# Two attention layers of a 1-core block: jobs in pairs, a bias by matmuls, products between the runs

## The chip, the core and the metric

One NeuronCore of a Trainium2 chip runs the whole program. Its engines work side by side and meet through semaphores: PE (TensorE, matmuls and transposes into PSUM), DVE (VectorE), ACT (ScalarE), POOL (GpSimd) and SP (SyncE, which here issues the loads). The metric is the time of one execution in microseconds of the device, as the median of several runs. Lower is better.

## What is computed

Two blocks follow each other on 512 tokens of width 1024: a first block (a gated mixer, a recurrent mixer, and a mixture of experts behind each), then a second block of two layers. The change touches the attention of the second block's two layers. Shortened to it:

```python
h = rmsnorm(x, ln1_g[i]) @ w_in[i]
(fq, fk, fv, ff, dq, dk, dv, c_q, c_kv, k_r) = jnp.split(h, split_points, axis=-1)
# third kind of jobs below: 4 heads of 64, causal, decay bias cum[q] - cum[k]
logf = log_sigmoid(ff + f_bias);  cum = jnp.cumsum(logf, axis=1)
o_fox  = softmax(fq @ fk.T / 8 + where(k <= q, cum[q] - cum[k], NEG)) @ fv
# second kind: 4 heads, two score maps each (widths 64 and 64), values of 128
o1, o2 = softmax(q1 @ k1.T / 8 + alibi_and_chunk_mask) @ v, softmax(q2 @ k2.T / 8 + ...) @ v
o_diff = rmsnorm(o1 - lam * o2, norm_g) * (1 - lam_init)
# first kind: 4 heads of 64 + 32 rotated, chunk mask
o_mla  = softmax(q @ k.T * 96 ** -0.5 + chunk_mask) @ v
x = x + concatenate([o_fox, o_diff, o_mla]) @ w_o[i]
```

Everything is fp32. A feed-forward part follows each attention.

## The kernel before

The program is written out engine by engine. For each stage there is one function per engine (`tensor()`, `scalar()`, `vector()`, `gpsimd()` inside `attention`, L1792), and the order of the lines in it is the order of the engine's queue. Nothing is reordered by a scheduler. Results go from PE to the others through eight PSUM banks taken in turn (`Banks.take`, L131): PE waits there until the bank's last reader has released it.

**Dense products.** Weights arrive as raw fp32 units, and each half of a unit is split into a high part (ACT, L263) and a low part (DVE or POOL, L271), six halves ahead. A product (L593 with features as output rows, L595 with tokens as output rows) is then three matmuls for each piece. In the attention they are, by the names of their keys: `mla` (L528), `dq`, `dk`, `dv`, `fv`, `fqk`, and `atto`, the product with `w_o` in two column halves (`(atto, 0)` at L595, `(atto, 1)` at L615).

**Jobs.** A job is one head, one query block of 128 and, in the second kind, one of the two maps. The blocks come in the order `BLOCKS = (3, 1, 2, 0)`, and block `qc` sees keys in `128 * (qc + 1)` columns. There are 16 jobs of the first kind (`mla`), 32 of the second (`diff`), 16 of the third (`fox`). A job is
- scores: one fp32 matmul of 96 rows (first kind) or 64 rows (the others), L1870;
- DVE adds the bias and scales while it copies the scores out of PSUM (L2063), then takes the maximum (L2064);
- ACT takes the exponential and its sum (L1964);
- PE transposes the result (L1876), ACT copies it to SBUF (L1972), PE multiplies with the values (L1884);
- DVE scales by the reciprocal sum (L2069, and L2077, L2081 and L2083, or L2086).

`pipeline` (L1847) runs the jobs of one kind with a lag of three: on PE the transposes of job m-3, the scores of job m, the values of job m-4. Each kind has its own run, which fills and drains. `dv` stands inside the second kind's run. `fv` and `fqk` stand between the second and the third run.

**The third kind's bias.** The forget logits come as four extra columns of `fv`. After that product DVE takes their log-sigmoid (L743) and PE sums it up over tokens (L1927, 20 short matmuls). The sums are turned to a row (L1935), and for each head a matmul with 4 rows spreads them over the partitions (L1867). ACT copies that, adds the query's own sum (L1961), POOL masks the diagonal block (L2173), and only then DVE adds it to the scores. L501 turns finished output columns to features for the last product; ACT and DVE split them (L506, L513).

**The second kind's norm** is on ACT 16 squares (L2023) and a root (L406), and on DVE 16 scalings (L2136) and 4 more (L2143), placed between the second and third run, in DVE's queue ahead of the log-sigmoid.

## Time and profile before

| | us |
|---|---|
| median of 3 runs | 2784.52 (2782.84 to 2785.44) |
| the profiled execution, its own time | 2782.48 |
| its span | 2781.3 |

| engine | busy us | share of the span |
|---|---|---|
| PE, matmuls | 2669.2 | 96% |
| PE, weight loads | 1851.0 | 67% |
| DVE | 1220.8 | 44% |
| ACT | 928.7 | 33% |
| POOL | 368.2 | 13% |

### The profile page before, as it was taken

What the parts mean: (1) busy time and instruction counts of PE and PEld (TensorE: products, weight loads), DVE (VectorE), ACT (ScalarE), POOL (GpSimd) and SP (SyncE); (2) the same over time, 40 slices, a digit from 0 to 9 for tenths busy, and PEclk for the clock granted to TensorE, in tenths of its full rate; (3) what the DMA queues carried; (4) which work ended last, traced back from release to release, by engine and by line L of the source; (5) the groups of instructions that cost most, each with busy time, mean ns of one, the idle gap of its engine ahead of it and who ended that gap; (6) DMA issues with size and microseconds to landing.
All of it is one profiled execution on the core that took longest, in us unless ns stands there. A gap on an engine that the chain in (4) does not pass through costs nothing. (4 is left out here: it accounts for less than half of the span.)

```text
span 2781.3 us, 33208 instructions
## 1 busy us (share of the span) xinstructions
PE 2669.2 (96%) x13232; PEld 1851.0 (67%) x13232; DVE 1220.8 (44%) x2353; ACT 928.7 (33%) x1770; POOL 368.2 (13%) x197
## 2 busy tenths in 40 slices
PE   7989999999978999999799999999999999999999
PEld 6865444454856444544487768888888776888887
DVE  2542232333655232322445733562554573356254
ACT  4431111112373111111345543442344554344233
POOL 3200000001230000000120111221222011122122
PEclk9999999999989999999999969999999995999999
DMA  5139999998215999999621001322132100132212
GB/s 210 64 125 411 421 421 421 421 421 346 76 46 218 420 421 421 421 421 421 249 88 61 32 30 61 107 95 87 61 110 94 61 33 30 61 106 94 89 61 83
DMA packets 136893, 543.62 MB, mean 195 GB/s; under 512 B 16672, under 2 KB 28192, under 8 KB 87456
## 3 DMA queue, kind: packets, MB, share of 16 engines
q1 hardware_dynamic: 127120, 536.94, 49.2%
q10 hardware_dynamic: 9616, 4.51, 0.6%
q8 instruction: 108, 1.77, 0.3%
q14 instruction: 49, 0.40, 0.0%
HBM read 539.32 MB, written 2.10 MB: 195 GB/s over the span
## 5 line engine op out<-in xcount | busy, mean ns | idle before, releaser
L593 PE MATMUL ps<-w,w 128*128 128x512 f32 x2976 | 678.8, 390 | 2.6 <-POOL w L271 2.6
L593 PEld LDWEIGHTS ps<-w,w 128*128 128x128 f32 x2976 | 558.2, 188 | 120.0 <-POOL w L271 3.4
L271 POOL TENSOR_TENSOR w<-w,w 128x1024 fp32r<-128x1024 f32 (+3 forms) x139 | 335.7, 2425 | 2152.8 <-ACT w L263 2152.8
L1345 PE MATMUL ps<-w,w 128*64 128x512 f32 x2048 | 451.6, 594 | 1.8 <-issue 1.8
L595 PE MATMUL ps<-w,w 128*128 128x512 f32 (+1 forms) x1872 | 413.5, 383 | 17.4 <-issue 15.2
L595 PEld LDWEIGHTS ps<-w,w 128*128 128x128 f32 x1872 | 342.3, 190 | 86.6 <-issue 19.9
L263 ACT ACTIVATE w<-w 128x1024 fp32r<-128x1024 f32 (+3 forms) x260 | 252.4, 999 | 414.3 <-PE ps L595 182.0
L271 DVE TENSOR_TENSOR w<-w,w 128x1024 fp32r<-128x1024 f32 (+3 forms) x121 | 192.5, 1597 | 371.1 <-ACT w L263 368.7
L1345 PEld LDWEIGHTS ps<-w,w 128*64 128x64 f32 x2048 | 146.0, 137 | 285.6 <-issue 285.6
L1597 DVE TENSOR_TENSOR X<-ps,X 128x512 f32<-128x512 f32 x256 | 163.0, 682 | 163.3 <-PE ps L1381 162.3
L1367 PE MATMUL ps<-w,w 128*64 128x512 f32 x1024 | 226.8, 595 | 0.8 <-ACT w L1431 0.8
L2281 DVE SCALAR_TENSOR_TENSOR w<-ps,PK,w 128x511 f32<-128x511 f32 (+1 forms) x176 | 131.9, 749 | 75.5 <-ACT w L2237 72.4
L1367 PEld LDWEIGHTS ps<-w,w 128*64 128x64 f32 x1024 | 70.6, 137 | 139.8 <-issue 138.9
L1884 PEld LDWEIGHTS ps<-w,w 128*128 128x128 f32 x640 | 97.8, 224 | 56.9 <-ACT w L1972 28.0
L1320 PE MATMUL ps<-w,w 128*128 128x256 f32 x1024 | 130.8, 287 | 4.9 <-DVE w L1568 4.9
L1320 PEld LDWEIGHTS ps<-w,w 128*128 128x128 f32 x1024 | 129.7, 195 | 7.6 <-DVE w L1568 5.1
L1585 DVE TENSOR_TENSOR w<-ps,w 128x512 f32<-128x512 f32 x32 | 34.8, 1086 | 212.0 <-PE ps L1345 212.0
L615 PE MATMUL ps<-w,w 128*128 128x512 f32 x528 | 122.0, 390 | 0.0
L1884 PE MATMUL ps<-w,w 128*128 128x64 f32 (+1 forms) x640 | 115.5, 321 | 4.6 <-ACT w L1972 4.1
L1380 PE MATMUL ps<-w,w 128*128 128x512 f32 x256 | 111.9, 437 | 4.6 <-DVE w L1604 4.6
L1604 DVE SCALAR_TENSOR_TENSOR w<-ps,w,w 128x512 fp32r<-128x512 f32 x64 | 45.1, 747 | 159.0 <-ACT w L1476 159.0
L615 PEld LDWEIGHTS ps<-w,w 128*128 128x128 f32 x528 | 98.8, 188 | 20.3
(247 smaller groups left out, 2505.5 us busy)
## 6 DMA issues: line engine op xcount, KB each, us to landing
w<-in_moe_w_gate SPq DMA_DIRECT2D x128, 1024.0 KB, 13.9
w<-in_moe_w_up SPq DMA_DIRECT2D x128, 1024.0 KB, 16.6
w<-in_moe_w_down SPq DMA_DIRECT2D x128, 1024.0 KB, 13.1
w<-in_w_up SPq DMA_DIRECT2D x40, 1024.0 KB, 5.1
w<-in_w_down SPq DMA_DIRECT2D x20, 1024.0 KB, 5.0
w<-in_w_in SPq DMA_DIRECT2D x16, 1024.0 KB, 5.0
w<-in_ab_w_in SPq DMA_DIRECT2D x10, 1024.0 KB, 5.2
w<-in_c_w_in SPq DMA_DIRECT2D x8, 1024.0 KB, 5.0
```

What stands on the lines that cost most here:

```text
L263: up(self.whi, self.S.e.activation(hi, raw, ACT.Copy))
L271: up(self.wlo[self.low[s][0]], lane.e.tensor_tensor(lo, raw, hi.bitcast(F32), ALU.subtract))
L593: ins = pe.matmul(bank[:, :], wp[:, k, P * o:P * o + P], ap(k0 + k), start=first, stop=stop)
L595: ins = pe.matmul(bank[:, 0:width], ap(k0 + k)[:, P * o:P * o + P], wp[:, k, :], start=first, stop=stop)
L615: ins = pe.matmul(bank_of(o)[:, 0:width], ap(k)[:, P * o:P * o + P], wp, start=(k == 0 and pi == 0), stop=(hi is rows[-1][0] and pi == 2))
L1320: i = pe.matmul(bank[:, 256 * k:256 * k + 256], HB[part][:, c, t:t + P], SELR[:, c, :], start=(part == 0 and c == 0), stop=(part == 1 and ...
L1345: ins = pe.matmul(bank[64 * e:64 * e + 64, :], XG[p % 3][:, 4 * u + k, 64 * e:64 * e + 64], w[e][:, k, :], start=(u == 0 and k == 0), stop ...
L1367: ins = pe.matmul(two[n][64 * e:64 * e + 64, :], HDT[:, 2 * u + k, 64 * e:64 * e + 64], w[e][:, k, 512 * n:512 * n + 512], start=(u == 0 a ...
L1380: pe.matmul(bank[:, :], s_, YH[:, 512 * n:512 * n + 512], start=True, stop=False)
L1597: up(bx.free, dve.tensor_tensor(x, bank[:, :], x, ALU.add))
L1884: ins = pe.matmul(bank[:, 0:dv], PTB[m % 2][:, P * j:P * j + P], vals(j), start=(j == 0), stop=(j == qc))
L2281: ins = dve.scalar_tensor_tensor(y[:, d:T], bank[:, 0:T - d], col("conv_w_2", 132 * i + 44 * tap + f), y[:, d:T], ALU.mult, ALU.add)
```

## The change

1. **Two jobs at a time.** `pipeline` goes in steps of two jobs: the values of job 2p-5, the transposes of 2p-4 and 2p-3, the scores of 2p and 2p+1, the values of 2p-4. The two score matmuls follow each other. In the second kind the two are the two maps, in rows 0 to 63 and 64 to 127. The third kind's jobs are reordered so that a pair is two heads, in the same two row halves. The first kind's pairs use 96 rows each.
2. **One run for the first two kinds**, with `dv` at step 10 and `fqk` at step 24, after the last scores of the second kind and before its last transposes and values.
3. **The third kind's bias by matmuls.** The sums are written as three bf16 parts each, with ones beside them, turned to rows once for all heads, and a bf16 matmul of 6 rows adds `cum[q] - cum[k]` into the same PSUM bank as the scores. A bf16 matmul of the identity with a causal block of 0 and -1e30 adds the mask. ACT scales the queries by 1/8 as it copies them. DVE takes the maximum straight from PSUM and ACT the exponential straight from PSUM. L1867, L1935, L1961, L2173 and the third kind's part of L2063 are gone.
4. **The forget logits ride with `mla`** (420 columns, a second small load of 16 KB for each unit). Log-sigmoid and sums come before `dk`; the parts are made by DVE before it splits `dk`'s next weights; 8 bf16 transposes and one ACT copy follow the transposes of the first kind.
5. **Products between.** `fv` (256 columns) stands at step 2 of the third kind. The norm of the second kind is in DVE's queue ahead of that step. Six output features are turned in steps 3 to 5. The last three steps of the third kind stand in the middle of `(atto, 0)`, whose row halves are taken in the order (1, 0), while four PSUM banks are held.

```diff
+            for p in steps:
+                if p in at_step:
+                    at_step[p]()
+                if first_values:
+                    values_of(2 * p - 5)
+                for m in (2 * p - 4, 2 * p - 3):
+                    if 0 <= m < len(jobs):
+                        turn(m0 + m, jobs[m])
+                if 2 * p < len(jobs):
+                    scores(m0 + 2 * p, jobs[2 * p:2 * p + 2])
+                if not first_values:
+                    values_of(2 * p - 5)
+                values_of(2 * p - 4)
...
+        def two_kinds(engine, dv, fqk):
+            n = M_FOX // 2
+            pipeline(mla_jobs + diff_jobs, 0, engine, {M_DIFF // 2 + 2: dv, n: fqk}, range(n + 3))
+
+        def third_kind(engine, fv, o_feature):
+            at_step = {2: fv}
+            for n in range(3):
+                at_step[3 + n] = lambda n=n: o_feature(FEATURES_OUT[2 * n:2 * n + 2])
+            pipeline(fox_jobs, M_FOX, engine, at_step, range(len(fox_jobs) // 2))
...
-            bank = banks.take(bsc)
-            n = P * (qc + 1)
-            up(bsc.full, pe.matmul(bank[:, 0:n], q, k[:, 0:n], start=True, stop=True))
+            taken = [banks.take(kind) for _ in two]
+            for bank, (qc, _, _, q, k, _, _) in zip(taken, two):
+                n = P * (qc + 1)
+                ins = pe.matmul(bank[:, 0:n], q, k[:, 0:n], start=True, stop=not fox)
+                if not fox:
+                    up(bsc.full, ins)
+            if fox:
+                for bank, (qc, _, h, _, _, _, _) in zip(taken, two):
+                    n, of_head = P * (qc + 1), slice(32 * h, 32 * h + 6)
+                    pe.matmul(bank[:, 0:n], turned_q[of_head, P * qc:P * qc + P], turned_k[of_head, 0:n],
+                              start=False, stop=False)
+                for bank, (qc, _, _, _, _, _, _) in zip(taken, two):
+                    n = P * (qc + 1)
+                    up(bfs.full, pe.matmul(bank[:, n - P:n], CTB[:, 0, :], CTB[:, 1, :], start=False, stop=True))
...
+            def rest(unit):
+                if unit == 1:
+                    banks.held = bx.banks[-NT:]
+                    rest_of_third(engine)
+                    PE.wait_ge(bo.free, M_FOX + len(fox_jobs))
+                    tensor_o_features(FEATURES_OUT[6:])
+                    banks.held = ()
...
+            if kind == "fox":
+                bank = bfs.next(V)
+                up(mx, dve.tensor_reduce(AT[:, m % 8:m % 8 + 1], bank[:, 0:n], AX, ALU.max, negate=True))
+                return
```

On PE, in the second kind, before (L1870 scores, L1884 values, L1876 transposes; an `x2` is two matmuls in one row):

```order
L1870 MATMUL ps<-w_22528_11034,w_20480_11032 128x512
L1884 MATMUL ps<-w_16384_11035,w_14336_11026 128x128 x3
L1876 MATMUL ps<-CT,w_12288_11025 128x128
L1870 MATMUL ps<-w_22528_11034,w_20480_11032 128x512
L1884 MATMUL ps<-w_16384_11035,w_14336_11026 128x128 x3
L1876 MATMUL ps<-CT,w_12288_11025 128x128
```

And now (L1924 scores, L1954 values, L1946 transposes):

```order
L1924 MATMUL ps<-w_22528_11038,w_20480_11036 128x512 x2
L1954 MATMUL ps<-w_16384_11039,w_14336_11030 128x128 x6
L1946 MATMUL ps<-CT,w_12288_11029 128x128 x2
L1924 MATMUL ps<-w_22528_11038,w_20480_11036 128x256 x2
L1954 MATMUL ps<-w_16384_11039,w_14336_11030 128x128 x2
```

The two maps' scores now stand next to each other, and so do their values and transposes.

On PE, around the last scores of the third kind and the middle of `(atto, 0)`, now (L1930 the bias of 6 rows, L1934 the mask, L602 a dense product, w_20480 queries and keys, w_22528 the third kind's values):

```order
L1924 MATMUL ps<-w_20480_11042 128x128 x2
L1930 MATMUL ps<-junk 128x128 x2
L1934 MATMUL ps<-CTB 128x128 x2
L1954 MATMUL ps<-w_22528_11043,w_14336_11030 128x64 x2
L602 MATMUL ps<-w_32768_62,w_0_74 128x512
...
L1954 MATMUL ps<-w_22528_11043,w_14336_11030 128x64 x2
L1946 MATMUL ps<-CT,w_12288_11029 128x128 x6
L1954 MATMUL ps<-w_22528_11043,w_14336_11030 128x64 x6
L1946 MATMUL ps<-CT,w_12288_11029 128x128 x2
L1954 MATMUL ps<-w_22528_11043,w_14336_11030 128x64 x2
L508 MATMUL ps<-CT,w_8192_11028 128x128 x8
```

48 of `(atto, 0)`'s 96 matmuls stand between the third kind's last scores and its drain; before, all 96 followed the drain.

On DVE, from the last jobs of the second kind to the first of the third, before (L412 to L2143 the norm, L271 weight splits, L2146 on the log-sigmoid):

```order
L2081 TENSOR_TENSOR AT<-AT,LS 128x1
L2083 SCALAR_TENSOR_TENSOR w_8192_11024<-ps,AT,w_18432_11036 128x128
L412 RECIPROCAL SM<-SM 128x16
L2136 SCALAR_TENSOR_TENSOR w_8192_11024<-w_8192_11024,SM,dnB 128x128 x16
L2143 TENSOR_SCALAR w_8192_11024<-w_8192_11024 128x512 x4
L271 TENSOR_TENSOR w_37888_70<-w_28672_51,w_36864_64 128x1024
L271 TENSOR_TENSOR w_41984_72<-w_30720_52,w_40960_66 128x1024
L2146 TENSOR_TENSOR sb_cum<-w_22528_11039,fgB 128x16
```

And now (L2145 maxima of the third kind, L419 to L2261 the norm, L277 weight splits, L2166 reciprocals):

```order
L2178 TENSOR_TENSOR AT<-AT,LS 128x1
L2180 SCALAR_TENSOR_TENSOR w_8192_11028<-ps,AT,w_18432_11040 128x128
L2145 TENSOR_REDUCE AT<-ps 128x1 x4
L419 RECIPROCAL SM<-SM 128x16
L2254 SCALAR_TENSOR_TENSOR w_8192_11028<-w_8192_11028,SM,dnB 128x128 x16
L2261 TENSOR_SCALAR w_8192_11028<-w_8192_11028 128x512 x4
L277 TENSOR_TENSOR w_33792_68<-w_24576_49,w_32768_62 128x1024
L277 TENSOR_TENSOR w_37888_70<-w_26624_50,w_36864_64 128x1024
L2166 RECIPROCAL AT<-AT 128x1 x2
L2145 TENSOR_REDUCE AT<-ps 128x1 x2
```

The log-sigmoid has left this place; four maxima of the third kind stand before the norm, and the maxima of its third pair behind it and behind two weight splits.

## Rows read from the trace of the kernel before

**Rows 1.** The page: span, PE, and the slices' granted clock in tenths.

```profile
span 2781.3 us, 33208 instructions
PE 2669.2 (96%) x13232; PEld 1851.0 (67%) x13232; DVE 1220.8 (44%) x2353; ACT 928.7 (33%) x1770; POOL 368.2 (13%) x197
PEclk9999999999989999999999969999999995999999
```

**Rows 2.** Busy time by stretch: stretch, length, engines, granted clock, DMA share, GB/s.

```profile
1466.02:1491.29 25.27, 22.90 (x153) 17.72 (x153) 19.29 (x63) 16.00 (x49) 0.00 (x0) 1.00 0.14 51
1491.29:1514.83 23.54, 23.54 (x103) 18.61 (x102) 6.40 (x12) 6.33 (x12) 1.30 (x1) 1.00 0.12 45
1514.83:1568.96 54.13, 53.30 (x298) 35.95 (x299) 42.75 (x138) 30.78 (x92) 2.36 (x1) 1.00 0.07 20
1568.96:1602.22 33.26, 33.26 (x194) 29.51 (x194) 22.33 (x54) 17.89 (x50) 7.38 (x3) 1.00 0.27 94
1602.22:1609.09 6.87, 4.54 (x42) 4.20 (x40) 3.36 (x8) 3.72 (x7) 2.37 (x1) 1.00 0.24 56
1609.09:1668.83 59.74, 57.50 (x177) 36.54 (x177) 22.43 (x67) 28.05 (x72) 4.67 (x16) 0.54 0.03 13
1668.83:1692.15 23.32, 23.32 (x97) 19.16 (x97) 4.99 (x6) 3.18 (x3) 2.39 (x1) 0.93 0.14 46
```

**Rows 3.** The second layer's last two stretches; ten microseconds of the first's third kind.

```profile
2304.27:2364.01 59.74, 56.60 (x176) 35.68 (x177) 22.42 (x67) 28.05 (x72) 4.67 (x16) 0.55 0.03 10
2364.01:2387.89 23.88, 23.88 (x96) 19.58 (x97) 4.98 (x6) 3.18 (x3) 2.39 (x1) 0.91 0.14 45
...
1640.00:1650.00 10.00, 10.00 (x26) 5.08 (x25) 3.32 (x12) 5.12 (x14) 1.00 (x4) 0.50 0.00 1
```

**Rows 4.** Who waited for whom on PE, 1461 to 1670 us.

```profile
PE ps L1867 <- DVE tr L2158: 2.3, 1, 2.3
...
PE ps L1876 <- ACT w L1964: 1.4, 1, 1.4
...
PE ps L595 <- DVE w L513: 0.7, 1, 0.7
```

**Rows 5.** PE's timeline where the first kind's run begins.

```profile
1461.49 3.65 PE L501 MATMUL ps<-CT,w 128*96 128x128 f32 x32
1466.02 2.17 PE L1870 MATMUL ps<-w,w 96*128 96x512 f32 x6 [0.87 <-DVE w L2128]
```

**Rows 6.** One head of each kind: first kind, then second, by stretch.

```profile
1476.30:1481.83 5.53, 5.53 (x40) 4.34 (x39) 4.89 (x17) 3.83 (x13) 0.00 (x0) 1.00 0.01 3
...
1524.38:1538.45 14.07, 14.07 (x77) 9.22 (x77) 11.83 (x38) 7.81 (x25) 0.00 (x0) 1.00 0.01 2
```

**Rows 7.** PE's timeline: a lone score matmul, and three at the run's start.

```profile
1524.38 1.12 PE L1870 MATMUL ps<-w,w 64*128 64x512 f32 x2
1525.43 0.82 PE L1884 MATMUL ps<-w,w 128*128 128x128 f32 x5
...
1491.29 1.55 PE L1870 MATMUL ps<-w,w 64*128 64x512 f32 x6
1492.77 22.06 PE L595 MATMUL ps<-w,w 128*128 128x512 f32 x96
```

**Rows 8.** DVE's groups in the second kind's head: busy, mean, idle before, releasers.

```profile
L2063 DVE SCALAR_TENSOR_TENSOR w<-ps,w 128x512 f32<-128x512 f32 (+3 forms) x8 | 3.9, 489 | 1.8 <-PE ps L1870 1.5 <-DVE w L2051 0.2
```

**Rows 9.** PE's timeline: the sums ahead of the third kind.

```profile
1602.22 2.29 PE L1927 MATMUL ps<-sb_cum,CT 128*128 128x4 f32 x20
```

**Rows 10.** The page's kind of group, whole trace, shapes apart: a small bf16 matmul.

```profile
L1331 PE MATMUL ps<-w,w 128*128 128x128 bf16 x128 | 12.4, 219 | 0.0
```

**Rows 11.** DVE's timeline: end of the rotation, and the norm.

```profile
1460.41 0.64 DVE L2122 COPY w<-w 128x128 f32<-128x128 f32 x4
...
1576.31 0.25 DVE L412 RECIPROCAL SM<-SM 128x16 f32<-128x16 f32 x1 [6.49 <-ACT SM L406]
1576.60 8.58 DVE L2136 SCALAR_TENSOR_TENSOR w<-w,SM,dnB 128x128 f32<-128x128 f32 x16
```

More of the change, by code:

```diff
@@ L193, in add @@
             self.n_dense += 1
-        self.count[slot] += 16 * len(parts)
+        self.count[slot] += 16 * sum(len(pieces) for _, _, pieces in parts)
         u = Unit(len(self.units), parts, split, len(self.halves), slot, self.count[slot], self.holder[slot])
@@ L1862, in tensor_scores, with pipeline, values_of @@
-        def tensor_scores(m, job):
-            qc, kind, h, q, k, _, _ = job
-            if kind == "fox" and qc == BLOCKS[0]:
-                PE.wait_ge(crow, 1)
-                bank = banks.take(ba)
-                up(ba.full, pe.matmul(bank[:, :], cst("sel")[0:4, P * h:P * h + P], CROW[0:4, :], start=True, stop=True))
-            bank = banks.take(bsc)
-            n = P * (qc + 1)
-            up(bsc.full, pe.matmul(bank[:, 0:n], q, k[:, 0:n], start=True, stop=True))
+        def pipeline(jobs, m0, engine, at_step, steps):
+            scores, turn, values = engine
+            first_values = turn is tensor_turn
+            def values_of(m):
+                if 0 <= m < len(jobs):
+                    values(m0 + m, jobs[m])
+            for p in steps:
[4 more added lines that the diff above has]
+                for m in (2 * p - 4, 2 * p - 3):
+                    if 0 <= m < len(jobs):
+                        turn(m0 + m, jobs[m])
[4 more added lines that the diff above has]
+                values_of(2 * p - 4)
@@ L1929, in tensor @@
             up(bv.full, ins)
-            PE.wait_ge(o_done, 4)
-            tensor_o_features((6, 7, 2, 3))
-            PE.wait_ge(cum, 2)
-            bank = banks.take(bv)
-            for c in range(NT):
-                ins = pe.transpose(bank[0:4, P * c:P * c + P], CU[:, c, :], ident)
-            up(bv.full, ins)
-            PE.wait_ge(ba.free, 30 + 8)
-            pipeline(fox_jobs, M_FOX, tensor_scores, tensor_turn, tensor_values, lambda: tensor_o_features((4, 5)))
-            PE.wait_ge(bo.free, M_FOX + len(fox_jobs))
@@ L1940, in tensor @@
-            tensor_o_features((0, 1))
-            place = {k: n for n, k in enumerate((6, 7, 2, 3, 4, 5, 0, 1))}
-            def ready(k):
-                PE.wait_total(bf.free, mark["o"] + 1 + max(place[x] for x in range(k)))
-            tensor_out(("atto", i), H, ready, ahead=lambda: tensor_half(next_rows, 0))
-        def scalar_scores(m, job):
+            tensor_product(("dk", i), ALL4, 512, H, ba, feature=True)
+            PE.wait_ge(q1k1, 1)
+            tensor_features(lambda c, h: Q1[:, c, 96 * h:96 * h + 96], 4, lambda k: bv if k % 2 else ba, rows=96)
@@ new lines, in tensor @@
+            tensor_features(lambda c, h: K1[:, c, h, :], 4, lambda k: bv if k % 2 else ba, rows=96)
+            PE.wait_ge(cum_parts, 1)
+            PE.wait_total(ctb, 2)
+            bank = banks.take(ba)
+            for j in range(2):
+                for c in range(NT):
+                    ins = pe.transpose(bank[:, :].bitcast(BF16)[:, T * j + P * c:T * j + P * c + P], CM6[:, j, c, :], CTB[:, 0, :])
+            up(ba.full, ins)
+            PE.wait_ge(ba.free, 10 + 8 + 4 + 4)
+            PE.wait_ge(bv.free, 2 + 4)
@@ L1950, in scalar_scores, with scalar_exp @@
+            tensor_out(("atto", i), [lambda k, f=f: f(ROWS_OUT[k]) for f in H], ready, rest,
+                       ahead=lambda: tensor_half(next_rows, 0))
+        def scalar_scores(m, two):
+            scalar_exp(m, two[0])
+            scalar_exp(m + 1, two[1])
+        def scalar_exp(m, job):
             qc, kind, h = job[0], job[1], job[2]
             n = P * (qc + 1)
+            p = PB[m % (LAG + 1)]
+            scores = p
             if kind == "fox":
-                if qc == BLOCKS[0]:
-                    bank = ba.next(S)
-                    S.wait_ge(fox_m, 4 * h)
-                    bank_to(NB, bank[:, :])
-                    S.wait_total(ba.free, ba.free.n)
@@ L1958, in scalar_scores @@
[L1958 to L1962 removed]
+                scores = bfs.next(S)
+                S.wait_ge(bpt.full, m - LAG)
             S.wait_ge(mx, m + 1)
[L1964 to L1965 removed]
+            up(bfs.free if kind == "fox" else ex,
+               act.activation(p[:, 0:n], scores[:, 0:n], ACT.Exp, bias=AT[:, m % 8:m % 8 + 1],
+                              accum_out=AT[:, 8 + m % 8:9 + m % 8]))
@@ L2450, in constants @@
     put("pri8", np.tile(8 - np.arange(8, dtype=np.float32), (P, 1)))
-    sel = np.zeros((4, 4, P), np.float32)
-    for h in range(4):
-        sel[h, h, :] = -1.0
-    put("sel", sel.reshape(4, 512))
+    put("causal", np.where(j <= p, 0.0, NEG).astype(np.float32))
     return c
```

246 lines of the change are left out of this document (137 added, 109 removed).

## The prediction, made before the run

> **What bounds the kernel now.** I read the page first: PE is busy 96% of 2781.3 us, and its clock row shows two dips in the second half [rows 1]. Everything the change moves lies in two stretches, one for each layer, so the next view is the busy time by stretch, from the first kind's first scores to the end of `(atto, 0)` and the first part of `(atto, 1)` [rows 2]. The seven stretches sum to 226.1 us. The reader is to see that PE is busy for nearly all of each, and that one stands out: 59.74 us for the third kind at a granted clock of 0.54, in the second layer 59.74 us at 0.55 [rows 3]. Within it, 10.00 of 10.00 us are busy at 0.50: PE is the bound there, at half speed. DVE and ACT are busy 22.43 and 28.05 us of it. In the other kinds PE is the bound at full clock: a head of the second kind takes 14.07 us with PE busy throughout and DVE 11.83 us, a head of the first 5.53 us with DVE 4.89 us [rows 6]. PE's waits are short [rows 4].
>
> **Start of the runs: +3.2 us a layer.** The 20 sum matmuls (2.29 us [rows 9]) now stand ahead of `dk`; they are taken out again below, so only the place changes. What is new is on DVE. Its rotation ends at 1461.05 [rows 11], just before PE's turns at 1461.49 [rows 5], and behind it now come a copy, three memsets and nine small steps, by DVE's small steps of about 0.2 us some 3 us, and only then two weight splits and the four copies for which PE waits 0.87 us [rows 5]. PE comes there 2.2 us later than before, so about 1 us more is seen, and with it 8 bf16 transposes (0.1 us each by 12.4/128 [rows 10]). Bounds: +0.5 to +3 beside the 2.2. I take 1.0. The log-sigmoid goes into a time in which DVE waits for PE: nothing. Queued behind it are DVE's splits for `dk`, needed 20 us later. The extra 16 KB loads go through SP's queue well ahead: nothing. POOL loses 16 masks, and two casts at the start hide in its wait for weights.
>
> **First and second kind: -10.3 us a layer.** Do two fp32 matmuls of 64 rows in different halves really run together? The old order has this once: three score matmuls (512, 512 and 256 columns) take from 1491.29 to 1492.77, 1.48 us, where a lone 512 takes 1.05 us [rows 7]. In sequence they would take 1.05 + 1.05 + 0.5 = 2.6. So the second one costs almost nothing. A head has 2 x 1280 columns, by 1.05 us for 512 some 5.3 us; half, 2.6, goes, and some 0.1 us of change-over for each job: 2.9. PE would need 11.2 us. But DVE has its own work: of the 14.07 us it waits 1.5 for scores [rows 8], so it needs 12.6. DVE becomes the bound, and the gain is 1.5 a head, 6.0 a layer (bounds: 0 if the longer loop of two jobs makes PE and DVE wait for each other, 11.6 if PE stayed the bound). The first kind's pairs have 96 rows and can't run together; its 5.53 stays. Its drain goes: the stretch has 25.27 - 22.90 = 2.4 us of idle time [rows 2], 1.4 of it at the start, which stays; 1.0 goes. The second kind's drain (last 3.3 us of its 54.13, behind the last scores) moves behind `fqk` and is counted there. Together 6.0 + 1.0 + 3.3.
>
> **From `fv` to the end of the 96th `atto` matmul: -30.1 us a layer.** Before: 33.26 + 6.87 + 59.74 + 23.32 = 123.2 us [rows 2]. After, on PE, all at full clock:
> Dense work: 33.26 + 22.4 = 55.7 (the 23.32 had some 0.9 us of half clock).
> The second kind's drain: 3.3, and about 1.9 more since ACT first empties `fqk`'s banks and splits a weight half: 5.2.
> The third kind's scores: four heads of 1280 columns in pairs, 2 x 2.6, and change-overs: 5.9. Transposes and values are those of the first kind: 5.53 less its scores (1280 columns at 1.05 for 512, less 0.1 each: 2.3) is 3.2 for a head, four times 13.0.
> The added bias and mask. A dense product streams 512 columns in 22.06/96 = 0.23 us [rows 7]; 5120 bias columns are then 2.3 us if each runs alone. 16 mask matmuls of 128 columns are 1.6 us by 0.10 each [rows 10]. Bounds 2.7 (pairs of bias matmuls together) to 6 (each at the fp32 rate). I take 3.9, as these are bf16.
> Eight turned features, by 3.65/8 = 0.46 us each for 4 transposes [rows 5]: 3.7.
> Changing between 128, 64 and 32 rows: a lone 64-row score costs 0.1 us more than a 96-row one would; two or three changes for each of 8 steps: 2.0.
> Waits: PE behind ACT's copies of `fv` 1.1; scores of step 3 behind step 2's exponentials, whose maxima wait on DVE behind the norm, 0.5; in the middle of `(atto, 0)` for copies 1.0; for the last values and features 1.1 as before (0.7 of it in [rows 4]): 3.7.
> Sum: 55.7 + 5.2 + 5.9 + 13.0 + 3.9 + 3.7 + 2.0 + 3.7 = 93.1.
> Gone from the path are the sums (2.3), the row and the spreading matmuls, the wait of 2.3 us behind them [rows 4], and above all the half clock.
> The norm is the place to watch. Before, `fqk` hid it. Now squares and root on ACT (DVE waited 6.49 us for them), then 8.58 us and four smaller scalings on DVE [rows 11] and two splits stand ahead of the maxima of step 2: about 19 us after the drain. PE has 3.1 us of scores, 11.5 of `fv`, 1.1 of waiting and 3.5 of step 2: the cover is just long enough. If `fv` were not there, 10 us would show.
>
> **The sum.** 3.2 - 10.3 - 30.1 = -37.2 for the first layer. In the second the last stretch is 0.6 us longer, at half clock for longer [rows 3]: -37.8. Together -75.0, from the profiled execution's own 2782.5: 2707.5. The median of the runs is 2 us above that execution, so I forecast **2710 us**.
>
> **A rule of the skill against the rows.** The third kind stays at 0.50 for 10 us in which PE is never idle [rows 3]. Behind that stands what the Trainium skill says (TensorE: Matmul & The Clock Gate, "What's actually happening"): the throttled state is the default and activity releases it. By that rule the full clock would be sure after the change, as PE stays busy; the trace does not agree that being busy is enough. The first kind, with much the same matmuls, keeps 1.00 [rows 2].
>
> **Rivals.**
> A. *The third kind falls to the half clock again.* For: before, it is entered at 1.00 and loses it after short matmuls of 4 columns or 4 rows and a wait of 2.3 us; in the second layer with less waiting too. Against: it now comes out of 22 us of `fqk`, is cut by `fv` and `(atto, 0)`, has no 4-row matmuls, and is like the first kind. From step 2 to 7 PE has about 19 us of work; doubled, less 2 us of waits that vanish: +17 a layer, 2743 us. In one layer only: 2726. 20%.
> B. *No gain from pairs.* The loop is longer (maximum of both, exponential of both, then transposes), or the matmuls don't run together in this stream, which is also how the change could fail to do what it says. Then 6.0 of the jobs and 2.6 of the third kind's scores don't come, and waits of 2 us do: 10.6 a layer, 2730. Speaks against: [rows 7]. 12%.
> C. *More than forecast:* DVE's 12.6 has slack in it (it is busy 11.83), bias pairs run together, fewer change-overs: 0.8 x 4 + 1.2 + 1 + 1 = 6 a layer, 2697. 9%.
> D. *Slower.* The clock is lost at the start of the first kind's run, behind 40 transposes and a longer wait for DVE, and PE then goes on at 0.50. First kind 22 more, the second kind from `dv` on 22.2 us a head against 12.6, in some 3.5 heads 34 more, third 17: 73 against 38 gained, 35 a layer, 2853 us. It decides as soon as more than 38 us of PE's full-clock work a layer run at half. The rows speak against: from 1461.49 on PE turns 32 blocks and waits 0.87 and 1.4 us, and the clock stays 1.00 [rows 2, 4, 5]. The Trainium skill (same page, "Part 4: PE-mode transpose") says that full clock does not engage in transpose mode; by that rule the added transposes would count for D, and the trace so far does not bear it out there. 4%.
>
> **How the numbers follow.** Forecast 55%, A 20%, B 12%, C 9%, D 4%. The forecast's own bounds (start +2, jobs 3 either way, bias -1.2 to +2 a layer) reach from 2699 to 2725. With A, B and C the range is 2695 to 2745; D is out, and the far ends of A and B with it. All but D are faster by far more than 0.2% (5.6 us, about what a measurement of this kernel can tell from no change): faster 95%, within 0.2% 1%, slower 4%.
>
> **What the profile of the changed kernel will show.** A head of the second kind near 12.6 us with DVE idle for less than 0.5 and PE idle now and then, each pair of 512 columns in about 1.1 us; the first scores about 3 us later after `dk`; the third kind at 1.00, some 22 us of PE between `fv` and `(atto, 0)`; no wait above 2 us at step 2 or 3. I am wrong if PEclk still dips there (A), if the head stays near 14 us (B), or if PE waits long for DVE's maxima behind the norm.

## The result, and the profile after

| | us |
|---|---|
| before, median of 4 runs | 2784.57 (2782.84 to 2785.44) |
| after, median of 4 runs | 2748.92 (2748.84 to 2750.51) |
| ratio | 0.9874, 95% interval 0.9857 to 0.9891 |
| forecast | 2710, range 2695 to 2745 |

The change made the kernel 35.6 us faster, where 75 were forecast; the time lies 4 us outside the range. In what follows, *before* and *after* are the two kernels and the traces of their profiled executions. That of after has a span of 2749.0 us against 2781.3 [rows 1].

These lines of after's page answer to [rows 1]. Both dips of PEclk in the second half are gone:

```profile
span 2749.0 us, 33272 instructions
PE 2610.8 (95%) x13288; PEld 1825.9 (66%) x13288; DVE 1201.3 (44%) x2337; ACT 910.1 (33%) x1740; POOL 361.4 (13%) x167
PEclk9999999999989999999999999999999999999999
```

The first layer's stretches in after answer to [rows 2]: first kind up to `dv`, `dv`, second kind up to `fqk`, `fqk`, drain and first third-kind scores, `fv` to the last scores, `(atto, 0)` with the third kind's rest. Columns as there (length; PE, PEld, DVE, ACT, POOL busy; granted clock; DMA):

```profile
1472.09:1502.81 30.72, 25.30 (x158) 18.72 (x159) 22.22 (x68) 18.65 (x54) 0.00 (x0) 1.00 0.10 36
1502.81:1526.44 23.63, 23.63 (x98) 19.07 (x97) 3.41 (x9) 5.75 (x10) 2.40 (x1) 0.93 0.13 44
1526.44:1580.42 53.98, 43.06 (x272) 31.09 (x271) 36.94 (x121) 28.77 (x82) 1.27 (x1) 0.91 0.07 21
1580.42:1602.32 21.90, 21.90 (x100) 18.11 (x99) 3.45 (x10) 5.00 (x10) 1.29 (x1) 1.00 0.15 49
1602.32:1609.75 7.43, 6.26 (x45) 4.12 (x44) 3.46 (x12) 4.45 (x18) 2.35 (x1) 1.00 0.24 73
1609.75:1647.88 38.13, 35.38 (x263) 29.44 (x262) 24.67 (x65) 26.73 (x79) 5.63 (x2) 0.91 0.20 70
1647.88:1679.07 31.19, 29.58 (x134) 24.20 (x134) 7.89 (x20) 6.39 (x13) 2.37 (x1) 0.89 0.11 34
```

The third kind has left the half clock: 0.91 where [rows 2, 3] have 0.54 and 0.55. But in the second kind PE was busy for 53.30 of 54.13 us before; now it is idle for 11 of 53.98 us. The prediction's three terms, by the starts of the same operations in both traces:

| term | forecast | layer 1 | layer 2 |
|---|---|---|---|
| `mla` to the first scores | +3.2 | +4.2 | +4.1 |
| first and second kind, with `dv` | -10.3 | +5.4 | +4.4 |
| `fqk` or `fv` to the 96th `atto` | -30.1 | -24.5 | -27.7 |

With 1.9 us lost before the first layer's attention this makes -32.2; the spans differ by -32.3. (The other 3.3 of the 35.6 are how each profiled execution lies to its median.) The middle row is the failed step.

Who waited for whom on PE in after's first layer, 1472 to 1681 us (columns: us in total, times, longest). Before, the only waits above a microsecond were 2.3 and 1.4 [rows 4]:

```profile
PE ps L1946 <- DVE w L2180: 8.8, 8, 1.8
PE ps L1946 <- ACT w L2048: 3.8, 7, 1.1
PE ps L1946 <- DVE w L2183: 3.1, 5, 1.3
```

L1946 is the transpose of a job's exponentials, and L2180 and L2183 are DVE scaling *values*. A transpose needs no values. What it needs is a PSUM bank. PE's timeline where a head of the second kind begins, layer 2 of after:

```profile
2230.23 1.13 PE L1924 MATMUL ps<-w,w 64*128 64x512 f32 x4
2231.29 1.60 PE L1954 MATMUL ps<-w,w 128*128 128x128 f32 x12
2232.73 0.27 PE L1946 MATMUL ps<-CT,w 128*128 128x128 f32 x1
2234.77 0.30 PE L1946 MATMUL ps<-CT,w 128*128 128x128 f32 x1 [1.77 <-DVE w L2180]
2235.00 0.70 PE L1924 MATMUL ps<-w,w 64*128 64x256 f32 x4
```

and DVE's in the same time (L2160 bias, L2161 maximum):

```profile
2233.49 0.69 DVE L2161 TENSOR_REDUCE AT<-w 128x1 f32<-128x512 f32 x1
2234.09 0.15 DVE L2178 TENSOR_TENSOR AT<-AT,LS 128x1 f32<-128x1 f32 x1
2234.28 0.35 DVE L2180 SCALAR_TENSOR_TENSOR w<-ps,AT,w 128x128 f32<-128x128 f32 x1
...
2235.74 0.43 DVE L2160 SCALAR_TENSOR_TENSOR w<-ps,w 128x256 f32<-128x256 f32 x1 [0.72 <-PE ps L1924]
```

A step takes six banks of the eight in turn: values 2p-5, transposes 2p-4 and 2p-3, scores 2p and 2p+1, values 2p-4. Eight takes before the second transposes lie the values of job 2p-7. PE takes the values of 2p-5 at the *start* of a step; the code has DVE scale them at the *end* of its step, behind both score tiles. So PE's transpose at 2234.77 waits for DVE's end at 2234.63, and DVE then waits 0.72 us for PE's next scores: they go in turns. In the next two steps of this head PE waits for DVE again at the same place, 1.22 and 0.63 us; in the fourth its wait is one of 0.34 us for ACT. The theory BANK of the runs below is this loop.

### The profile page after: what moved, and what is told of

Read it like the earlier page. It is cut to its first block, busy times and chain, and to the rows that moved or that the text cites. A ratio compares the mean times of both kernels' runs of the same rounds, so it can differ in the third digit from the quotient of the medians.

```text
span 2749.0 us, 33272 instructions
## 1 busy us (share of the span) xinstructions
PE 2610.8 (95%) x13288; PEld 1825.9 (66%) x13288; DVE 1201.3 (44%) x2337; ACT 910.1 (33%) x1740; POOL 361.4 (13%) x167
## 4 chain that ended last, share of the span: by engine, by line
PE 88%; DVE 6%; issue 3%; ACT 2%; DMA 0%; POOL 0%; SPq 0%; DVEq 0%; ACTq 0%
PE ps L600 24%; PE ps L1362 16%; PE ps L602 14%; PE ps L1384 8%; PE ps L1337 5%; PE ps L622 4%; PE ps L534 3%; PE ps L1397 3%; PE ps L1398 2%; PE ps L1924 1%; PE ps L1954 1%; DVE w L2160 1%; PE ps L535 1%; PE ps L1946 1%; PE ps L452 1%
## 5 line engine op out<-in xcount | busy, mean ns | idle before, releaser
L600 PEld LDWEIGHTS ps<-w,w 128*128 128x128 f32 x2976 | 560.2, 188 | 120.2 <-POOL w L277 3.4
L277 POOL TENSOR_TENSOR w<-w,w 128x1024 fp32r<-128x1024 f32 (+2 forms) x139 | 337.7, 2439 | 2228.7 <-ACT w L269 2228.7
L602 PE MATMUL ps<-w,w 128*128 128x512 f32 (+1 forms) x1872 | 416.3, 384 | 17.8 <-issue 15.2
L602 PEld LDWEIGHTS ps<-w,w 128*128 128x128 f32 x1872 | 343.8, 191 | 86.8 <-issue 19.5
L269 ACT ACTIVATE w<-w 128x1024 fp32r<-128x1024 f32 (+2 forms) x260 | 252.7, 1001 | 436.1 <-PE ps L600 196.4
L277 DVE TENSOR_TENSOR w<-w,w 128x1024 fp32r<-128x1024 f32 (+2 forms) x121 | 201.6, 1674 | 387.7 <-ACT w L269 385.1
L1337 PE MATMUL ps<-w,w 128*128 128x256 f32 x1024 | 131.3, 288 | 4.9 <-DVE w L1585 4.9
L1337 PEld LDWEIGHTS ps<-w,w 128*128 128x128 f32 x1024 | 130.2, 196 | 7.6 <-DVE w L1585 5.1
L622 PEld LDWEIGHTS ps<-w,w 128*128 128x128 f32 x528 | 98.7, 188 | 20.3
L1493 ACT ACTIVATE w<-ps,w 128x512 fp32r<-128x512 f32 x64 | 40.6, 684 | 204.0 <-PE ps L1384 204.0
L534 PE MATMUL ps<-w,w 128*128 128x256 f32 x768 | 99.9, 294 | 8.3 <-POOL w L277 6.7
```

The costliest lines, as they stand in the source:

```text
L269: up(self.whi, self.S.e.activation(hi, raw, ACT.Copy))
L277: up(self.wlo[self.low[s][0]], lane.e.tensor_tensor(lo, raw, hi.bitcast(F32), ALU.subtract))
L534: return pe.matmul(bs[o][:, t], w[:, P * o:P * o + P], a(k)[:, t], start=first, stop=stop)
L600: ins = pe.matmul(bank[:, :], wp[:, k, P * o:P * o + P], ap(k0 + k), start=first, stop=stop)
L602: ins = pe.matmul(bank[:, 0:width], ap(k0 + k)[:, P * o:P * o + P], wp[:, k, :], start=first, stop=stop)
L622: ins = pe.matmul(bank_of(o)[:, 0:width], ap(k)[:, P * o:P * o + P], wp, start=(k == 0 and pi == 0), stop=(hi is rows[-1][0] and pi == 2))
```

## The experiments

Each kernel is the changed one with the edit shown, unless said otherwise; `...` stands for lines left out. Each quoted passage is what was expected before the run. Every median is that of the kernel's own runs; before stood at 2784.1 to 2785.0 beside them.

### Values first on DVE

```diff
-                if first_values:
-                    values_of(2 * p - 5)
+                values_of(2 * p - 5)
                 for m in (2 * p - 4, 2 * p - 3):
...
-                if not first_values:
-                    values_of(2 * p - 5)
                 values_of(2 * p - 4)
```

> The changed kernel, with one edit: DVE scales the values of job 2p-5 before it takes the scores of pair p, as PE does, in place of behind them. Theory BANK: PE's transposes of job 2p-3 need the PSUM bank of the values of job 2p-7 (eight takes earlier, six takes a step), and DVE releases that only behind its scores of pair p-1; so PE and DVE go in turns. With the edit the bank comes free some 2 us earlier: PE's waits of 11.9 us a layer for DVE at the transposes fall below 3, a head of the second kind goes from 15.1 to 16.6 us to 12.6 to 13.5, a head of the first from 6.8 to about 5.7, and the program from 2749 to 2729 to 2737 us. Rival LOOP: the exponential of a pair comes late whatever the banks do; then waits for ACT take the place and the time stays above 2745. Rival CLOCK: what is lost are spells at the granted clock 0.50; then heads change by less than 0.5 us unless the spells go.

Measured: **2716.37 us** (2714.65 to 2719.43), ratio to before 0.9753 (0.9736 to 0.9769). The heads of the second kind, after first (full clock), then this one:

```profile
2230.23:2245.35 15.12, 11.15 (x78) 7.94 (x77) 11.27 (x38) 8.20 (x24) 0.00 (x0) 1.00 0.00 1
```

```profile
sum 12.54, PE 10.59 PEld 7.96 DVE 11.31 ACT 7.91 POOL 0.00; mean PE 10.59 PEld 7.96 DVE 11.31 ACT 7.91 POOL 0.00
```

12.54 us, where the prediction said 12.6. These are the same instructions, in 2.6 us less a head. The waits for DVE at the transposes are gone; what is left are waits of the value matmuls (L1951) and one transpose (L1943) for ACT's copies and exponentials (layer 2, 2130 to 2260 us):

```profile
PE ps L1951 <- ACT w L2053: 9.3, 13, 1.5
PE ps L1943 <- ACT w L2045: 1.1, 1, 1.1
```

Moving one line of DVE's order takes 32.5 us off the program, more than the 12 to 20 that were expected, and most of the miss (38.9). In the traces 12.3 and 11.3 us of it lie in the first two kinds of the two layers, 4.1 and 2.0 from `fqk` to the 96th `atto` (the third kind has the same order of values), and 1.6 in the second layer's `dk`, which the edit does not touch: in this execution it ran at full clock.

### Own banks, DVE's order left alone

```diff
...
+            banks.own = {bsc: [0, 1, 2], bpt: [3, 4], bo: [5, 6, 7]}
             two_kinds(engine, values_of_diff, queries_of_fox)
+            banks.own = None
```

> The changed kernel, with DVE's order as it was, but in the run of the first two kinds scores take three PSUM banks of their own in turn, transposes two and values three. Theory BANK: no transpose waits for DVE's values any more, the same gain as with the values first: 2729 to 2740 us. If it is the order on DVE that matters and not the bank (values that come late by themselves), no change: 2745 or more. Rival LOOP: no change either.

Measured: 2720.95 us (2713.92 to 2721.76), a head 12.48 us. Scores, transposes and values now take banks from rings of their own (the edit also lets `Banks.take` take from them). DVE still scales late, and the waits of the transposes for it are gone all the same; PE's longest waits are again those for ACT's copies, to the tenth as with the values first:

```profile
PE ps L1959 <- ACT w L2063: 9.3, 13, 1.5
```

So it is the bank, as BANK says, and LOOP falls. CLOCK falls with it, since the 15.12 us of after are a head at full clock. (The edit covers two of the three kinds.)

### Both maps in one row half

```diff
-DQ[64 * s:64 * s + 64, h, P * qc:P * qc + P], DK[64 * s:64 * s + 64, h, :]
+DQ[0:64, h, P * qc:P * qc + P], DK[0:64, h, :]
```

> The changed kernel, with both maps of the second kind read from rows 0 to 63 (the second map's queries and keys are left out and the first's taken twice), so that the two score matmuls of a pair can't run side by side. Theory: a pair of 512 columns goes from 1.06 to about 2.0 us, 2.4 us a head more on PE, and since PE's scores lie in the loop with DVE nearly all of it shows: 8 to 10 us a layer, 2765 to 2769 us. Rival (side by side is worth nothing, as DVE is the bound): under 3 us a layer, below 2755.

> The kernel with the values first, and both maps of the second kind read from rows 0 to 63 (the second map's queries and keys left out). In the run of before, PE was busy 10.59 us in a head of 12.54 and DVE 11.31 us. Without the overlap PE needs 2.1 to 2.4 us more: 12.7 to 13.0 us. Theory A: with the bank wait gone, side by side now counts: a head is 13.0 to 13.6 us, 2720 to 2726 us. Theory B: DVE bounds the head anyway and PE's added work lies in its idle time: the head stays within 0.2 us of 12.55, 2712 to 2719 us, with fewer spells at half clock as in the first pair of such runs.

Both kernels leave out the second map's queries and keys. In the changed kernel: 2739.44 us (2738.0 to 2741.34), **9.5 us faster** where 16 to 20 slower was expected. A head at full clock takes the same time, though PE has 2.1 us more to do:

```profile
sum 15.11, PE 13.27 PEld 9.26 DVE 11.26 ACT 8.31 POOL 0.00; mean PE 13.27 PEld 9.26 DVE 11.26 ACT 8.31 POOL 0.00
```

I had put the pair's scores into the loop. Only the first of the two is in it: DVE starts 1.2 us behind the pair's start in both kernels, and comes to the second 1.3 us later, when that too is done. A pair of 512 takes 1.98 us here and 1.13 in after, so the overlap is real, and worth nothing to the head. What is faster is the clock. The granted clock of the whole execution is 0.984 to 0.987 in the four runs here and 0.976 to 0.979 in the four of after. In this trace all heads take 15.11 us and `dv` 22.04 and 22.05. In after `dv` took 23.6 us in both layers, and one head of each layer was longer; the one in layer 1:

```profile
1534.90:1551.52 16.62, 13.76 (x78) 9.89 (x77) 11.44 (x38) 8.21 (x24) 0.00 (x0) 0.79 0.00 0
```

About half of the gain lies behind the edited heads: from `fqk` to the 96th `atto` this kernel takes 95.1 and 93.6 us, after 98.7 and 96.5. Behind that stands the Trainium skill (TensorE: Matmul & The Clock Gate, "A second HAM failure mode: psum-queue depth-cycling"): in a bf16 kernel that cycles through banks, PE idles for moments between groups often enough that the clock oscillates. The rows agree in kind: 11.15 of 15.12 us busy and spells at 0.50 in some heads, against 13.27 of 15.11 and none in these heads. That less idle time is the cause of the kept clock is inferred from this pair, not isolated.

With the values first: 2719.26 us (2718.02 to 2722.23), a head 12.81 us with PE busy 12.59. Against 12.54 and 2716.37 the overlap is worth 0.27 us a head; the two kernels' runs overlap. To stand the matmuls in pairs took PE from 14.07 [rows 6] to 12.59 us a head, and to run them together took it to 10.59; the head saw little more than the first part. The Trainium skill says so too (TensorEngine Tiling (Array Packing), "PSUM Bottleneck"): packing speeds up TensorE, not the emptying of PSUM.

### One job at a time in the first two kinds

```diff
-            pipeline(mla_jobs + diff_jobs, 0, engine, {M_DIFF // 2 + 2: dv, n: fqk}, range(n + 3))
+            for m in range(n + 4):
...
+                if 3 <= m < n + 3:
+                    turn(m - 3, jobs[m - 3])
+                if m < n:
+                    scores(m, jobs[m:m + 1])
+                if m > 3:
+                    values(m - 4, jobs[m - 4])
```

> The changed kernel, with the jobs of the first two kinds one at a time again, in the order of the kernel before (transposes of m-3, scores of m, values of m-4), still one run, with dv at step 20 and fqk at step 48. Theory BANK: the pairs as built cost more than they give; heads go back to 14.07 and 5.53 us, and the program gains 5 to 7 us a layer: 2735 to 2740 us. Rival CLOCK (the heads lose time by half clock alone): it would lose the pairs' gain and be at 2755 or more.

Measured: 2728.48 us (2728.06 to 2730.38), 20.4 us faster than the change, more than the 9 to 14 expected; a head 14.08 us as before, the first kind's 5.53. Pairs as they were built cost 20 us; pairs with the values first gain 12 on top of one at a time.

### What the third kind's clock hangs on

Six runs, five of them on the kernel with the values first.

```diff
+            bank = banks.take(bv)
+            for c in range(NT):
+                for j in range(c + 1):
+                    ins = pe.matmul(bank[:, 4 * c:4 * c + 4], cst("trii") if j == c else cst("ones"), LF[:, j, :],
+                                    start=(j == 0), stop=(j == c))
+            up(bv.full, ins)
             third_kind(engine, values_of_fox, tensor_o_feature)
```

> The kernel with the values first, and the 20 sum matmuls of 4 columns repeated right in front of the third kind (their result is not used). Theory SHORT: these short matmuls, with the waits around them, lowered the clock before; the third kind again loses it: granted clock near 0.5 to 0.8 in the stretch from the third kind's scores to the middle of (atto, 0), and 2 to 12 us a layer beyond their own 2.2 us, 2725 to 2745 us. Rival RUN: what kept the old third kind at half clock was its own stream of 4-row, 64-row and 128-row matmuls, unbroken for 60 us, once it had fallen; with fv at step 2 the clock is back soon: 2.2 to 3.5 us a layer, 2721 to 2724 us.

2717.78 us (2716.87 to 2718.21), 1.4 us more, below what either theory expected. The matmuls' own 2.2 us a layer come mostly out of waits that PE had behind them: from the third kind's first scores to `(atto, 0)` it is idle for 0.5 us in place of 2.7, at a granted clock of 1.00 in both layers. SHORT falls, at least with `fv` two steps behind: 20 matmuls of 4 columns ahead of the third kind don't take the clock away.

```diff
-            at_step = {2: fv}
+            at_step = {0: fv}
+            if norm:
+                at_step[2] = norm
```

> The kernel with the values first, and fv in front of the third kind's run (step 0 in place of 2), with the norm of the second kind left at step 2. By the prediction's sentence on the cover, about 10 us of PE's wait for the norm then shows at the transposes of steps 2 and 3, less the 1.6 and 0.7 us that are there now: 7 to 9 us a layer, 2730 to 2735 us. If ACT and DVE are through with the norm earlier than estimated, under 3 us a layer: below 2722. If the unbroken run of the third kind loses the clock too, over 12 us a layer: above 2740.

2724.50 us (2721.65 to 2729.63): 8 us, 4 a layer, below the 7 to 9 expected. The cover is needed, but for less than the 10 us that the prediction named: PE's waits at steps 2 and 3, for ACT's exponential and for the last instruction of DVE's norm, are 1.8 and 1.5 us. Unbroken, the pairs keep most of the clock (0.94 and 0.89 in the two layers).

```diff
-cst("sel")[0:4, P * h:P * h + P], CROW[0:4, :]
+cst("sel")[:, P * h:P * h + P], CROW[:, :]
...
+            vstep(dve.memset(CROW[:, :], 0.0))
```

(on the kernel before)

> The kernel before, with one edit: the matmul that spreads a head's row over the partitions (third kind) uses 128 rows, of which 124 hold zeros, in place of 4; DVE clears the operand first (under 1 us a layer). Theory ROWS: matmuls with 4 of 128 rows in use count little as activity, and they pull the third kind to half clock; then its granted clock is 0.9 or more in place of 0.54, and the two layers gain 20 to 28 us each: 2730 to 2745 us. Rival STREAM: single 64-row scores with values of 64 columns and the waits between them do it; the clock stays near 0.54: 2783 to 2787 us.

2784.88 us against 2784.06, ratio 1.0003 (0.9994 to 1.0013). ROWS falls, as far as rows that hold zeros can test it; the third kind is still at half clock:

```profile
1640.00:1650.00 10.00, 10.00 (x28) 5.95 (x28) 4.05 (x15) 5.35 (x16) 0.88 (x3) 0.50 0.00 1
```

```diff
-            pipeline(fox_jobs, M_FOX, engine, at_step, range(len(fox_jobs) // 2))
+            one_at_a_time(engine, {2 * p: f for p, f in at_step.items()}, range(len(fox_jobs)))
```

> The kernel with the values first, and the third kind's jobs one at a time (transposes of m-3, scores of m, values of m-4), in the same order of jobs, with fv and the features at the same places. If it is the pairs, side by side, that keep the clock up in the third kind, its stretch behind fv falls to 0.5 to 0.7 for most of it: 8 to 15 us a layer more, 2732 to 2746 us. If the pairs don't matter for the clock, only the overlap and the change-overs are lost: 1 to 4 us a layer, 2718 to 2724 us.

> The same with fv in front of the third kind, so that this comes close to the old third kind: one at a time, behind a dense product, unbroken up to (atto, 0); what it lacks of the old one are the spreading matmul, the row turned ahead, and the wait behind it. If pairs and breaks stand for each other, this falls to the half clock where neither of the two did alone: granted clock below 0.7, 2740 us or more. If the clock stays near 1.00, 2722 to 2732 us, what pulled the old one down is in its spreading matmuls or the waits and short matmuls in front.

`one_at_a_time` is the loop of the kernel before. With `fv` in its place: 2744.91 us (2743.20 to 2746.47), 28.5 more than in pairs. That is the number the first theory asked for, and yet the theory is wrong: behind `fv` the clock is 1.00. A part of the time is a wait of 5.2 us a layer that pairs don't have: one at a time, the first job's transposes stand ahead of `fv` and wait for its exponential. `fv` itself then runs in part at half. From the third kind's first scores to `(atto, 0)` it takes 53.0 and 52.9 us against 39.0 and 37.4. Layer 2, `fv`, and from there to the last scores:

```profile
2283.57:2298.00 14.43, 14.06 (x98) 13.86 (x97) 8.81 (x25) 5.16 (x10) 2.40 (x1) 0.82 0.08 20
2298.00:2324.41 26.41, 26.30 (x167) 17.85 (x168) 12.79 (x40) 14.88 (x42) 2.35 (x1) 1.00 0.20 70
```

With `fv` in front as well: 2755.02 us, and runs from 2749.19 to 2763.45, the widest spread of all. Its third kind, layer 2, then layer 1:

```profile
2291.00:2331.41 40.41, 39.94 (x193) 24.73 (x192) 23.04 (x68) 20.44 (x55) 3.26 (x2) 0.79 0.16 53
...
1602.90:1654.43 51.53, 51.06 (x188) 32.63 (x188) 22.66 (x68) 20.56 (x53) 2.34 (x1) 0.59 0.13 42
```

The same instructions in one execution, 11 us apart. So pairs alone keep most of the clock (0.94 and 0.89), and the break by `fv` alone gives it back behind `fv` (1.00); without both it falls, in one layer for nearly all of it (1612 to 1655 at 0.50 to 0.61), in the other for a part. This is the old third kind's state [rows 3]. Why this stream of 64-row scores loses the clock and the first kind's [rows 2] does not stays open.

```diff
-                    pe.matmul(bank[:, 0:n], turned_q[of_head, P * qc:P * qc + P], turned_k[of_head, 0:n],
-                              start=False, stop=False)
```

> The kernel with the values first, with the bias matmuls of 6 rows left out of the third kind (its bias is left out; the mask stays). By the prediction's term they cost 2.3 us a layer if each runs alone at the dense rate, 1.1 if pairs run together: the time is 2 to 4.6 us below 2716, 2711 to 2714. If PE waits there anyway, or they lie beside something, under 1 us a layer. If the clock needs them, longer than 2716.

2717.53 us (2716.86 to 2717.82), 1.2 us more. In the trace PE waits more instead (1.9 for 1.6 at the scores, 1.3 for 0.7 behind `fv`). The bias matmuls cost nothing that can be measured; I had charged 2.3 us a layer.

### A kernel that beats both

The head of 12.54 us is not DVE's bound after all:

> The kernel with the values first, and the bias tile of a head of the second kind (128x512, one instruction on DVE, 0.67 us and 0.27 us of waiting for itself) made by POOL in two instructions, a head or more ahead. Theory: DVE bounds the head at 12.55 us; it gets shorter by 0.7 to 0.95 us, so 2.8 to 3.8 us a layer less, 2708 to 2711 us. Rival: PE's and ACT's chain is the bound by then: under 1 us a layer, above 2714. A third: POOL slows DVE down while it works; then DVE's own instructions get longer.

```diff
-                vstep(dve.scalar_tensor_tensor(BT[:, h % 2, :], cst("dist"), -slopes[h], mask, ALU.mult, ALU.add))
+                V.wait_ge(tile_in, h + 1)
```

(POOL makes the tile in two instructions, queued behind its splits for `dk` and `dv`.) 2717.79 us (2714.66 to 2719.72), the head 12.55 us with DVE busy 10.74: no gain. DVE now waits 0.86 us for the head's first scores and starts on them 1.2 us behind the head's start, as it did with the tile; and PE has lost 1.50 us behind an ACT copy that stood in ACT's queue behind the second 512 exponential. So:

```diff
+                if turn is scalar_turn and 1 < p < len(jobs) // 2 and p + 1 not in at_step and p + 1 in steps:
+                    for k in range(2):
+                        scalar_exp(m0 + 2 * p + k, jobs[2 * p + k])
+                        turn(m0 + 2 * p - 2 + k, jobs[2 * p - 2 + k])
...
```

> The kernel with the values first, and on ACT, wherever no dense product stands between two steps, the copies of the next step's transposes come one behind each exponential (exponential of 2p, copy of 2p-2, exponential of 2p+1, copy of 2p-1) and not both behind both. Seen in the run with the tile on POOL: from 2204.60 DVE is never idle for 11.7 us, then waits 0.86 us for the next 512 pair, and PE had lost 1.50 us behind a copy that ACT made only behind the second 512 exponential. Theory ROUND: that turn of all three engines bounds the head of 12.55 us, not DVE; copies earlier take 0.3 to 1.0 us off a head (less here, since the tile's 0.94 us is still on DVE): 2710 to 2716 us. Rival: DVE is the bound: no change, 2716 or more.

2711.41 us (2710.30 to 2712.76), 5 us less; the second kind's head 12.31, the first kind's later heads 5.4 to 5.5 for 5.92, and PE's waits for these copies in the first two kinds 4.0 us (layer 2) for 8.1. Then all together, with the sums as four matmuls of 16, 12, 8 and 4 columns:

> Values first, tile on POOL, copies one behind each exponential, and the 20 sum matmuls as 4 wider ones. Theory ROUND: the head comes to 11.6 to 11.9 us, as DVE's own chain of 11.7 us is then the bound: 2.6 to 3.8 us a layer off; first kind up to 0.4 a head; sums 1.7 us a layer less. 2716 less 9 to 14: 2702 to 2707 us. If ROUND is wrong the tile again brings nothing, and only the sums' 3.4 us are seen: 2712 to 2714 us.

2711.63 us (2710.70 to 2712.21): no gain over the kernel with the copies alone, where 2702 to 2707 was expected. The head is 12.10, not 11.6 to 11.9. PE is through with sums and `dk` 3 us earlier (`dk` now at full clock), and stands and waits at the first scores:

```profile
PE ps L1927 <- DVE w L2248: 4.1, 1, 4.1
```

DVE's rotation, 20 groups of six instructions of 16 columns at 0.88 us a group, is what is late:

```diff
+                q4 = Q1[:, c, :].rearrange("p (h n) -> p h n", h=4)
+                for x1, x2, n in ((q4[:, :, 64:80], q4[:, :, 80:96], 4), (KR[:, c, 0:16], KR[:, c, 16:32], 1)):
...
```

> Values first, tile on POOL, copies one behind each exponential, sums as 4 wider matmuls, and DVE's rotation of the first kind's four heads in one set of instructions of 64 columns in place of four sets of 16. In the run without the last edit PE waited 4.1 us a layer for DVE in front of the first scores; DVE's rotation took 20 sets of 0.88 us. 12 sets fewer are some 10 us less on DVE, so this wait should go down to 0.9 or less: 3 to 3.7 us a layer, 2704 to 2706 us. If the wait is for something else on DVE's way (weight splits, copies), it stays above 2: 2709 or more.

**2704.62 us** (2703.55 to 2706.02), ratio to before 0.9712 (0.9696 to 0.9728), 44.3 us under the change. The wait is 0.4 us:

```profile
PE ps L1928 <- DVE w L2253: 0.4, 1, 0.4
```

## Why the prediction was right or wrong, step by step

**First and second kind (-10.3): wrong, the failed step.** The sentence was: "DVE becomes the bound, and the gain is 1.5 a head, 6.0 a layer". I summed each engine's own work and let the larger one bound the head. I did name the danger as a bound ("0 if the longer loop of two jobs makes PE and DVE wait for each other"), and closed the bounds at 0; it came out at -1 to -2.5 a head. I had both orders and the ring of eight banks in the code and didn't count the takes. The range then took 3 us a layer either way for the jobs, though those bounds leave 6 to the bad side. With the wait gone the head is 12.54 us, the stretch 96.1 us in both layers against 102.9 [rows 2]: -6.9 of the -10.3. Most of the rest is `dv` partly at half clock (1.2 and 1.5 us) and a first-kind head of 5.92 in place of 5.53. The clock's part differs between executions: `dv` took 23.3 and 23.5 us here and 22.03 in both layers with the sums again, where all up to it is the same.

**The reason for 12.6 was wrong too.** It is a round through PE, DVE and ACT. The kernel with the tile on POOL took 0.94 us a head off DVE (0.67 of work, 0.27 of waiting for its end) and gained nothing; with the order of ACT's copies changed instead the head fell to 12.31. That the number came out right is luck.

**What side by side is worth.** A pair in one row time: right (1.13 us for two of 512). That it would be seen: hardly, 0.27 us a head; the other 1.3 of the 1.5 that a head gained come without it. The 96-row pairs did not run together, as said: 512 and 256 columns take 1.29 us to the next matmul, and alone 0.95 and 0.44.

**Start of the runs (+3.2): the sums right, the rest by luck, 1 us small.** 4.2 and 4.1 us. The sums took their 2.2. The 1.0 for DVE's longer way and the bf16 transposes did not come: from the turns' start to the first scores it took 4.52 us for 4.53 before, as the transposes' 0.6 us lie in the old wait and PE then waits 0.42 us for DVE in place of 0.87. What came instead I had at nothing: 0.8 (layer 2: 0.7) from `mla`'s start to the sums, and `dk`, which took 23.67 us for 22.38, with the clock at 0.93 in the stretch around it. That clock is no fixed cost of the change: with the values first `dk` took 23.68 us in layer 1 and 22.04 in layer 2.

```profile
1440.00:1466.00 26.00, 26.00 (x116) 21.05 (x115) 20.66 (x137) 5.23 (x9) 2.40 (x1) 0.93 0.41 142
```

**`fqk` to the 96th `atto` (93.1 us): 98.7 and 96.5.** Drain 4.9 for 5.2, no wait above 1.6 us, clock mostly back: right. The third kind's own parts (scores to features, with waits) were to take 32.2 us and took 35.9 and 36.0. The same loop and spells at 0.50 (behind `fv` a granted clock of 0.87 in layer 2; 1629.3 to 1636.9 us of layer 1 at 0.55) are in it; with the values first they are 34.0 and 32.4 us and the whole 94.5 in both. In layer 1 another 2.2 us is the second half of `(atto, 0)`, 13.36 us for 11.16. Bias and mask (3.9) took 3.3 us of PE in layer 1; the eight turned features (3.7) took 5.4, four of them at the lower clock.

**Rivals.** A (third kind at half) did not come, but in spells of some 3 to 8 us a weak form of it came in the second and third kind, `dk` and `dv`, and it was right that this clock is fragile: the run with `fv` in front and one job at a time is A. B was the nearest: it had PE and DVE waiting on a longer loop, but at 2 us a layer where 11.9 were measured, so its 2730 was too low; its other half, matmuls that don't run together, did not come. Nor did C and D.

**Still uncounted:** 1.9 us were lost ahead of all this, in the program's first 51 us. PE's first product took 8.44 us for 7.41 and its second block 16.14 for 14.65, at a granted clock of 0.73 from 20 to 30 us against 0.83. The change adds only two casts on POOL there, and they are not shown to be the cause: all the kernels built on the changed one have them, and in three of their traces (one at a time in the first two kinds, the sums again, the tile on POOL) that block takes 14.66 us, in the others about 16.

## What to carry over

When an engine takes its buffers in turn from one ring, count the takes of a step before believing a sum of busy times: find who owned each buffer one round earlier, and where in the releaser's order its release stands. If a producer's step begins with what its consumer does last, they run in turns; write both in the same order. And after a wait is removed, read who is late next before paying for a faster engine: here a tile's 0.94 us a head off DVE, 3 us of sums and `dk` off PE, and the bias matmuls left out gave nothing by themselves. Only when DVE's rotation was shortened as well did PE's wait of 4.1 us at the first scores go.

## What the runs showed of the hardware

The granted clock can be worth more than the work. Two layers of one execution with the same instructions took 40.4 and 51.5 us at 0.79 and 0.59. PE with more to do (13.27 for 11.15 us in a head of 15.1) gave a program 9.5 us faster. And the order of the jobs and of one dense product moved the third kind between 0.59 and 1.00.

While POOL split a weight half, a DVE instruction of 16 columns with two inputs from SBUF was held to the end of it: 2.27 us in place of 0.17.

```profile
1453.86 0.17 DVE L2223 TENSOR_TENSOR w<-w,CT 128x16 f32<-128x16 f32 x1
...
1454.36 2.27 DVE L2220 TENSOR_TENSOR tr<-w,CT 128x16 f32<-128x16 f32 x1
```

```profile
1454.20 2.39 POOL L277 TENSOR_TENSOR w<-w,w 128x1024 fp32r<-128x1024 f32 x1 [20.67 <-ACT w L269]
```

This is the kernel with all but the rotation edit. The Trainium skill (SBUF — State Buffer, "SBUF: two separate sides") calls the pair of ports that DVE and POOL share an exclusive lock, held for the whole instruction, also against a DVE instruction with two inputs from SBUF; the rows agree.
